# Expert stage: silu rows are turned first in a step, and weighted outputs are added into the token rows by the scatter

## What is computed

```
scores = jax.nn.sigmoid(jnp.matmul(h, w_router, ...))
_, idx = lax.top_k(scores + b_router, TOP_K)
wts = jnp.take_along_axis(scores, idx, axis=-1)
wts = wts / jnp.sum(wts, -1, keepdims=True) * ROUTE_SCALE
...
def expert_block(acc, blk):
    tok, wt, e = blk
    yb = swiglu(h_pad[tok], w_e_gate[e], w_e_up[e], w_e_down[e]) * wt[:, None]
    return acc.at[tok].add(yb), None
...
return swiglu(h, w_sh_gate, w_sh_up, w_sh_down) + routed[:n]
```

## Time and profile before

| what | us |
|---|---|
| time, median of 3 runs (lowest, highest) | 4598.52 (4597.18, 4601.25) |
| time of the profiled execution | 4600.06 |
| its span, first to last instruction | 4598.2 |
| PE busy in the span | 3897.8 |
| DVE busy | 2492.4 |
| ACT busy | 1722.5 |
| POOL busy | 437.9 |

### The profile page before, as it was taken

The page is one execution under the profiler, slowest core; times in us unless marked ns, Lnnn a source line. Parts: engine busy times, 40 slices in busy tenths (PEclk is TensorE's granted clock), DMA queues, the critical chain, the costliest instruction groups (busy, mean ns, idle before and its releaser), DMA issues. The chain is left out here.

```text
span 4598.2 us, 46686 instructions
## 1 busy us (share of the span) xinstructions
PE 3897.8 (85%) x18351; PEld 3144.6 (68%) x18351; DVE 2492.4 (54%) x3841; ACT 1722.5 (37%) x2079; POOL 437.9 (10%) x295
## 2 busy tenths in 40 slices
PE   8677889669999999944399559789999999999999
PEld 1565767557777777733366447678888887888887
DVE  0334513458888888865643433359956663444444
ACT  0222512227777777732122023223233332222222
POOL 0001000014444444410000000000000000000000
PEclk9785879879999999976659779899999999999999
DMA  7210112326666666661002012224445555555554
GB/s 248 80 72 1 38 48 78 145 90 239 245 245 231 228 247 230 233 237 62 21 3 74 9 60 92 73 79 138 138 154 181 181 182 187 198 187 201 186 198 174
DMA packets 250053, 656.69 MB, mean 143 GB/s; under 512 B 44951, under 2 KB 144027, under 8 KB 206316
## 3 DMA queue, kind: packets, MB, share of 16 engines
q1 hardware_dynamic: 208508, 614.78, 37.9%
q0 software_dynamic: 41328, 38.93, 2.5%
HBM read 688.66 MB, written 125.31 MB: 177 GB/s over the span
## 5 line engine op out<-in xcount | busy, mean ns | idle before, releaser
L1503 DVE TENSOR_TENSOR w_lo<-w_raw,w_hi 128x2048 fp32r<-128x2048 f32 x288 | 651.6, 2290 | 172.4 <-ACT w_hi L1413 171.2
L1413 ACT ACTIVATE w_hi<-w_raw 128x2048 fp32r<-128x2048 f32 x288 | 539.3, 1907 | 7.2 <-DMA w_raw<-in_e_w,over_rows 4.3
L2362 DVE TENSOR_TENSOR w_lo<-w_raw,w_hi 128x2048 fp32r<-128x2048 f32 x128 | 293.2, 2290 | 351.1 <-ACT w_hi L2299 350.5
L2299 ACT ACTIVATE w_hi<-w_raw 128x2048 fp32r<-128x2048 f32 x128 | 245.3, 1916 | 523.0 <-DMA w_raw<-in_peer_u 274.9
L1144 PE MATMUL ps_peer<-peer_xT_hi,w_hi 128*128 128x512 f32 x1024 | 408.7, 399 | 4.1 <-DVE w_lo L2362 4.0
L1144 PE MATMUL ps_peer<-w_hi,coef_hi 128*128 128x512 f32 x1024 | 399.6, 390 | 6.1 <-DVE coef_lo L2459 6.1
L1146 PE MATMUL ps_peer<-peer_xT_hi,w_lo 128*128 128x512 f32 x1024 | 399.8, 390 | 0.0
L1145 PE MATMUL ps_peer<-peer_xT_lo,w_hi 128*128 128x512 f32 x1024 | 399.7, 390 | 0.0
L1145 PE MATMUL ps_peer<-w_lo,coef_hi 128*128 128x512 f32 x1024 | 399.3, 390 | 0.0
L1146 PE MATMUL ps_peer<-w_hi,coef_lo 128*128 128x512 f32 x1024 | 399.2, 390 | 0.0
L1626 PE MATMUL ps_gu<-w_hi,h2T_hi 128*128 128x512 f32 x792 | 311.0, 393 | 0.7 <-DVE w_lo L1503 0.7
(11 more groups left out here) (475 smaller groups left out, 7584.6 us busy)
## 6 DMA issues: line engine op xcount, KB each, us to landing
w_raw<-in_e_w SPq DMA_DIRECT2D x195, 1024.0 KB, 4.8
w_raw<-in_peer_u SPq DMA_DIRECT2D x64, 1024.0 KB, 5.9
w_raw<-in_peer_v SPq DMA_DIRECT2D x64, 1024.0 KB, 4.8
acts<-act_out SPq DMA_DIRECT2D x64, 512.0 KB, 6.6
gates<-gate_tile SPq DMA_DIRECT2D x8, 4096.0 KB, 15.3
act_back<-acts SPq DMA_DIRECT2D x64, 512.0 KB, 5.8
gates_back<-gates SPq DMA_DIRECT2D x64, 512.0 KB, 7.0
w<-in_w_in SPq DMA_DIRECT2D x26, 1024.0 KB, 7.4
```

What stands on the lines that cost most here:

```text
L1413: nc.scalar.activation(w_hi[:, slot(n), :], w_raw[:, slot(n), :], ACT.Copy).then_inc(hi_done.sem, 1)
L1503: nc.vector.tensor_tensor(w_lo[:, slot(n), :], w_raw[:, slot(n), :], w_hi[:, slot(n), :].bitcast(F32), ALU.subtract).then_inc(lo_done.sem, 1)
L2299: nc.scalar.activation(w_hi[:, n % 2, :], w[:, n % 2, :], ACT.Copy).then_inc(w_hi_done.sem, 1)
L2362: nc.vector.tensor_tensor(w_lo[:, n % 2, :], w[:, n % 2, :], w_hi[:, n % 2, :].bitcast(F32), ALU.subtract) \
```

## The change

1. **Order of a step.** `turn_hidden(b)` stands ahead of `gate_up(b + 1)` on PE, `hidden_high(b)` ahead of `out(b - 1)` and the two `high` on ACT, `hidden_low(b)` ahead of the two `low` on DVE.
2. **Weights of the tokens.** `wk` is computed on DVE in the routing part, right after `multiply(0)`, and stored by SP to a new scratch tensor `slot_weights`. Each `take` is followed by a second indirect transfer, which brings 128 weights of 4 bytes into a column of `block_weights` (`wslot`); `turn_x` waits for both. `out` multiplies by that column.
3. **The scatter adds.** The shared rows go to `expert_rows`, now 512 rows, one for each token; `put` of a routed block adds into them, indexed by `tok`. Since two adds may meet in a row, `put(b)` waits until `put(b - 1)` has landed.
4. **Combine** loads 512 rows once, multiplies by `gate_row` and adds x.

`hidden_hi` stands first, and `block_out` has a second input, the column of weights. The core of the diff:

```diff
@@ POOL
                     oob_is_err=False).then_inc(x_in[b % 4].sem, 16)
+                nc.gpsimd.indirect_dma_start(
+                    out=wslot[:, r:r + 1], out_offset=None, in_=scratch["slot_weights"],
+                    in_offset=bass.IndirectOffsetOnAxis(ap=vtab[:, r:r + 1], axis=0), bounds_check=V_PAD - 1,
+                    oob_is_err=False).then_inc(x_in[b % 4].sem, 16)
...
+                if b == T:
+                    pool.wait_ge(stored[0].sem, 32)
+                    pool.wait_ge(stored[1].sem, 32)
+                else:
+                    pool.wait_ge(stored[(b - 1) % NO].sem, 16 * ((b - 1) // NO + 1))
                 r = at_row[b - T]
                 nc.gpsimd.indirect_dma_start(
-                    out=scratch["expert_rows"], out_offset=bass.IndirectOffsetOnAxis(ap=vtab[:, r:r + 1], axis=0),
-                    in_=ob[:, b % NO, :], in_offset=None, bounds_check=V_PAD - 1, oob_is_err=False) \
+                    out=scratch["expert_rows"], out_offset=bass.IndirectOffsetOnAxis(ap=tok[:, r:r + 1], axis=0),
+                    in_=ob[:, b % NO, :], in_offset=None, bounds_check=S - 1, oob_is_err=False, compute_op=ALU.add) \
                     .then_inc(stored[b % NO].sem, 16)
@@ ACT
-                    nc.scalar.activation(ob[:, b % NO, h * S:(h + 1) * S], ps_d[:, h, :], ACT.Copy) \
+                    weight = 1.0 if b < T else wslot[:, at_row[b - T]:at_row[b - T] + 1]
+                    nc.scalar.activation(ob[:, b % NO, h * S:(h + 1) * S], ps_d[:, h, :], ACT.Copy, scale=weight) \
                         .then_inc(out_done.sem, 1)
...
             for b in range(T, NB):
+                hidden_high(b)
                 if b > T:
                     out(b - 1)
...
-                hidden_high(b)
@@ DVE, routing
             multiply(0)
+            link(nc.vector.tensor_tensor(sc[:], sc[:], mask[:], ALU.mult))
+            link(nc.vector.tensor_reduce(total[:, 0, :], sc[:], AX, ALU.add))
...
+            for t in range(T):
+                link(nc.vector.tensor_tensor(pick[:, 0], sel[:, 0, t, :].unsqueeze(1).to_broadcast([P, TOPK, E]),
+                                             iota8.unsqueeze(2).to_broadcast([P, TOPK, E]), ALU.is_equal))
...
+                ins = nc.vector.tensor_reduce(wk[:, t, :], pick[:, 1], AX, ALU.add)
...
             dve.wait_ge(route_act.sem, step["g0"])
@@ PE
             for b in range(T, NB):
+                turn_hidden(b)
                 if b + 1 < NB:
                     gate_up(b + 1)
-                turn_hidden(b)
                 if b + 3 < NB:
                     turn_x(b + 3)
                 down(b)
@@ combine
+            sp.dma_start(gate_row[:], scratch["gate_row"][0].partition_broadcast(P)).then_inc(rows_in.sem, 16)
+            for t in range(T):
+                sp.dma_start(rows[:, t, :], scratch["expert_rows"][t * P:(t + 1) * P, :]).then_inc(rows_in.sem, 16)
+            sp.dma_start(x[:], scratch["x_kept"].rearrange("(t p) d -> p t d", p=P)).then_inc(x_back.sem, 16)
...
+            dve.wait_ge(rows_in.sem, 16 * (T + 1))
             for t in range(T):
+                link(nc.vector.tensor_tensor(rows[:, t, :], rows[:, t, :], gate_row[:], ALU.mult))
+            dve.wait_ge(x_back.sem, 16)
...
+                nc.vector.tensor_tensor(x[:, t, :], x[:, t, :], rows[:, t, :], ALU.add)
```

More of the change, by code:

```diff
@@ L1522, in x_low @@
                                         x_hi[:, :, at].bitcast(F32), ALU.subtract).then_inc(xT_lo_done.sem, 1)
+            nc.vector.memset(wslot[:], 0.0)
             link(nc.vector.memset(ones[:], 1.0))
@@ L1734, in _ @@
                 down(b)
-    with nc.Block() as block:
+    core.drop(w_raw, w_hi, x_hi, h2, brow, wr, wr_hi, ones, scT, rank, flag, excl, so, lists, val, vtab, tok,
+              widx, sg, hid, h_hi, h_lo, ob, best, total, mask, wk, pick, wslot, sc, sel, rt)
+    rows = core.sb("token_rows", [P, T, D])
+    row, gate_row = core.sb("final_g", [P, D]), core.sb("gate_row", [P, D])
+    x_back, row_in, rows_in = core.sig("x_back"), core.sig("final_g_in"), core.sig("token_rows_in")
+    with nc.Block() as block:
+        @block.sync
+        def _(sp):
+            sp.dma_start(gate_row[:], scratch["gate_row"][0].partition_broadcast(P)).then_inc(rows_in.sem, 16)
+            for t in range(T):
+                sp.dma_start(rows[:, t, :], scratch["expert_rows"][t * P:(t + 1) * P, :]).then_inc(rows_in.sem, 16)
+            sp.dma_start(x[:], scratch["x_kept"].rearrange("(t p) d -> p t d", p=P)).then_inc(x_back.sem, 16)
+            sp.dma_start(row[:], a["final_norm_g"].partition_broadcast(P)).then_inc(row_in.sem, 16)
         @block.vector
```

82 lines of the change are left out of this document (26 added, 56 removed).

## The result

The changed kernel takes **4484.26 us** (median of 4 runs, 4482.73 to 4485.69), the kernel before beside it 4599.89 us (4597.18 to 4654.22). The ratio is **0.972, with a 95% interval of 0.965 to 0.979**. It compares means, and one of the four runs of before took 4654.22 us; by the medians it is 0.975. Forecast were 4470 us and a range of 4450 to 4535. The profiled execution after took 4484.45 us, its span is 4482.6 us, which is 115.6 us shorter than the 4598.2 us of before; the prediction's sum was -129.

What follows compares the result with a forecast made beforehand. PE was taken to bound the routed loop (busy 184.68 us of 200), DVE and ACT close behind. Terms -88 + 1 + 9 + 3 + 4 - 58 = -129 from 4600.06 give 4471, with the median 1.5 lower 4470; range 4450 to 4535.

Steps and rivals of the forecast that it cites:

- Step order: Routed loop: without PE's wait ahead of `down` a step falls from 10.40 to 9.46 us, -88 us over 94 steps.
- 0.6 us spare on the cycle: Routed step: the new chain over ACT and DVE lets PE start `turn_hidden(b + 1)` at 8.8 us; PE arrives at 9.46.
- First routed step: Start of the routed loop: `turn_hidden(4)` stands directly behind `gate_up(4)`, with silu and `multiply` between, +1 us.
- gather of weights: POOL, 95 more issues: hidden in the loop while POOL keeps up, late at its start; +3 us, between 1 and 8.
- The add costs nothing in the loop while it is below a step: Scatter in the loop: an add lands 6 to 7 us after issue, below the step of 9.46, so its wait is free.
- Routing: Routing chain on DVE: computing the weights of the tokens there costs +9 us, at least 8.4 and at most 10.9.
- End of the stage: Last two adds follow one another without cover; the last waits some 6 us and lands 2 us later itself: +4 us.
- combine: After the last scatter: fewer loads, four products and four sums on DVE; -58 us, between -52 and -62.
- The first: Loop: serial adds or POOL take back the step's gain; 4558 us, half of it 4515; chance 0.18.
- the third: Step: `multiply` comes later than PE, through longer links or a late `high`; step 9.8 us, +32, 4503; chance 0.13.
- The second: Loop: POOL becomes the bound, slower than before from a step of 10.84 us; 4661 at 11.5; chance 0.13.
- the forecast's own 4455 to 4490: Whole kernel: the total if the forecast holds and no rival occurs, likeliest 4470 us; chance 0.56.

Runs made afterwards that it cites:

- the complete kernel: Changed kernel with token weights computed where DVE sat idle, weights riding with the row gather (fetched two steps ahead), no weight gathers: 4453.17 us, ratio 0.971.
- the order alone: Kernel before with only the new order of a step on PE, ACT and DVE; plain scatters and combine as before: 4487.53 us, ratio 0.978.

## Why the prediction was right, and where it was not

- **Step order, -88.** Right in mechanism and nearly in size: 93.1 us alone. The step is 9.32 us, not 9.46, and the 0.6 us spare on the cycle were there: the wait for `hidden_lo` fell to 15.7 us, a little above the 15 named. What was read wrong is how much that spare is worth. It is all that a late over unit has left, and the prediction gave it to the column operand only.
- **First routed step, +1, and gather of weights, +3.** The second is the term that failed, by far. In the prediction's words it "is hidden while POOL keeps up". POOL keeps up, and it costs 26.3 us of loop all the same, or 22.6 in the complete kernel. The gather was judged by whether *it* is needed in time; the over unit that is queued behind it was not followed to its reader.
- **The add costs nothing in the loop while it is below a step.** Wrong in the same way. Its landing takes 7.9 us in the median against the 6 to 7 assumed, and a tenth took 9.4 or more, above the step of 9.32; its wait for the one before costs 4.2 us. But its longer issue and transfer cost 16.1. The sign that the prediction named, scatters that wait for a DMA, did appear (44.2 us) and turned out to be almost harmless.
- **Routing, +9.** It was +11.7, and 9.2 came back when the piece was moved to where DVE was idle. `route_excl` starts 8.9 us later, within the 8 to 11 named, and the other 3 us are behind it; profiles of the same routing differ by as much. That the wait for PE is absorbed was right: `route_excl` follows `hidden_low(0)` without one.
- **End of the stage, +4, and combine, -58.** Between the last scatter and the memset -53.6. The last add is issued 6.7 us behind the one before, against 4.45, and the next block starts 12 us after it, against 7.4. From there to the memset are 20 us, as worked out. Together it is 32.1 us where about 28 were named as the sign.
- **Rivals.** The first (the adds and POOL take the step's gain back) came true by a good quarter, 26 of 88 us; the third (a `high` waits for its transfer) is the form that it took. The prediction had them as two cases of which one may occur; they are one mechanism. The second (POOL the bound, slower than before) did not come in this kernel, but its price was real: moving the add raised the row gather from 1.3 to 2.0 us and the weight gather from 1.7 to 2.3, and one more wait in POOL's list made a kernel slower than the one before. Two of its sums are off by 1 us (4600 - 41 + 103 is 4662, and 32 above 4470 is 4502), which changes nothing.
- **The median** is 14 us above the forecast. A loss of 26 us in the loop, and of 2 to 3 each in the routing and at the end, is partly covered by the 18 us from the clock, which no part of the prediction contained. So the total was nearer than its terms, and that part is luck: without the 18 us it would have been near 4502, still in the range but outside the forecast's own 4455 to 4490.

The rule on contention that the prediction cited bears more weight than it gave it. The rows show it first: the same gather of 4 bytes a row takes 1.00 us at 1507.44 in the changed kernel, where a `low` starts 0.22 us later, and 2.45 us at 1527.43, 0.72 us into a `low` that ends at 1529.00; it is over 0.88 us behind that end, and a `low` takes 2.29 us in either kernel, so POOL alone pays. The Trainium skill ("SBUF — State Buffer", "Who interferes with whom") says that a DVE instruction with two SBUF inputs contends with a GpSimd instruction that reads SBUF. By that rule, the trace agrees, for the issue of indirect transfers too: `low` has two such inputs, and in this kernel an issue beside DVE's other instructions of the loop, with at most one, took its least. But the prediction read from the same section that this is no full block for descriptor writing, and there the measurement decides otherwise: an issue that starts inside a `low` waits for its end and is over a fixed 0.9 us behind it (an add 1.5).

## What to carry to other kernels

Ask of every transfer that is added to a queue not when its own data are needed, but who stands behind it and how much that one has to spare: here 95 gathers with three steps of slack made the loop 26 us longer through the one fetch that had the least. When an edit takes the spare time out of a step, price the other edits against the new step; the same additions cost 13 us with a step of 10.4 and 37 with one of 9.3. And a wait in an in-order queue must be for something that is long done: one step less of prefetch turned a kernel that was slower than before into the fastest of this study.

## What the hardware showed that was not expected

- A gather of 128 rows of 4 bytes costs POOL as much as one of 128 rows of 4 KB: 0.99 to 1.01 us at the least, 1.6 and 1.3 us on average, and 5.4 against 5.3 us to landing.
- An add in a scatter is issued in 1.55 us at the least (the plain one in 0.97) and lands after 7.9 us in the median against 5.5 with the order alone.
- The issue of an indirect transfer that starts while DVE is inside a 128x2048 fp32 `tensor_tensor` on two SBUF tiles stands still until this ends and finishes 0.86 to 0.93 us later (an add 1.47 to 1.51), in thirteen traces without exception; one that starts ahead of it takes its least. So a row gather costs 0.99 to 3.10 us by its start alone, and reordering a queue can cost more than the wait that it removes.
- An unchanged block took 2481 to 2503 us, in the order of the time that one stretch of it ran at a granted clock of 0.50 (58 to 99 us) before this returned to 1.00. Whether an edit's shift or the run decides this, the runs don't show.
